# Three transformer blocks on one core: residual held token-major, with norm roots as columns per token block

## What is computed

```python
# block 1: modulated pre norm (scale and shift from c), gated post norm
h = rms_norm(x, g_pre) * (1 + scale) + shift
h = (silu(h @ w_gate) * (h @ w_up)) @ w_down            # or a mixer
x = x + 0.5 * (1 + gate) * rms_norm(h, g_post)          # factor 1 for the mixer
# block 2: plain pre norm, post norm
x = x + 0.5 * rmsnorm(swiglu_2(rmsnorm(x, pre), w_gu, w_down), post)
# block 3, twice: pre norm only
x = x + hybrid(rms_norm_3(x, g_mix)) @ w_out
x = x + (silu(h2 @ w_gate) * (h2 @ w_up)) @ w_down      # h2 = rms_norm_3(x, g_ffn)
return rms_norm_3(x, g_final)
```

## Time and profile before

| | us |
|---|---|
| median of 3 runs | 3627.2 (3626.7 to 3627.62) |
| span of the profiled execution | 3626.8 |
| PE busy | 3478.4 (96%) |
| DVE busy | 1965.9 (54%) |
| ACT busy | 1124.9 (31%) |
| POOL busy | 153.6 (4%) |

### The profile page before, as it was taken

One profiled execution on the slowest core, in us unless ns is written; L12 is line 12 of the kernel. 1 busy time (PEld: TensorE's weight loads), 2 busy tenths in 40 slices (PEclk: granted clock), 3 DMA queues, 4 the chain that ended last, 5 costly groups with the idle time before them and its releaser, 6 DMA issues. The chain is left out here.

```text
span 3626.8 us, 45721 instructions
## 1 busy us (share of the span) xinstructions
PE 3478.4 (96%) x18518; PEld 2717.8 (75%) x18518; DVE 1965.9 (54%) x2658; ACT 1124.9 (31%) x1482; POOL 153.6 (4%) x127
## 2 busy tenths in 40 slices
PE   9999999999999999998799999999999999999998
PEld 7887776688878887677578886666788866568886
DVE  6667545622344333988553435795534358953334
ACT  2222334422232223342332223335322233542222
POOL 0000000000000000000000000330000022200000
PEclk7999999999999999999899999999999999999999
DMA  6554231122222222210022222210222221112221
GB/s 244 185 183 172 81 108 40 55 104 93 93 81 94 103 93 102 75 65 4 13 82 93 99 98 78 74 70 24 89 96 93 98 88 70 47 47 93 99 98 70
DMA packets 47231, 325.75 MB, mean 90 GB/s; under 512 B 5232, under 2 KB 5488, under 8 KB 8688
## 3 DMA queue, kind: packets, MB, share of 16 engines
q1 hardware_dynamic: 41792, 290.10, 22.4%
q0 software_dynamic: 5296, 33.61, 2.6%
HBM read 321.59 MB, written 2.10 MB: 89 GB/s over the span
## 5 line engine op out<-in xcount | busy, mean ns | idle before, releaser
L2107 PE MATMUL PS<-HH,WH 128*128 128x512 f32 x2264 | 895.5, 396 | 21.5 <-DVE HL L2531 15.9
L2108 PE MATMUL PS<-HL,WH 128*128 128x512 f32 x2264 | 884.1, 391 | 0.0
L2109 PE MATMUL PS<-HH,WL 128*128 128x512 f32 x2264 | 884.1, 391 | 0.0
L2513 DVE TENSOR_TENSOR WL<-RAW,WH 128x2048 fp32r<-128x2048 f32 x264 | 613.6, 2324 | 497.8 <-ACT WH L2366 497.5
L2366 ACT ACTIVATE WH<-RAW 128x2048 fp32r<-128x2048 f32 x264 | 503.0, 1905 | 297.4 <-PE PS L2109 289.5
L2107 PEld LDWEIGHTS PS<-HH,WH 128*128 128x128 f32 x2264 | 426.6, 188 | 140.3 <-issue 33.7
L2109 PEld LDWEIGHTS PS<-HH,WL 128*128 128x128 f32 x2264 | 426.6, 188 | 90.2
L2108 PEld LDWEIGHTS PS<-HL,WH 128*128 128x128 f32 x2264 | 427.0, 189 | 87.6 <-issue 1.4
L2107 PE MATMUL PS<-AH,WH 128*128 128x512 f32 x1056 | 412.5, 391 | 3.3 <-DVE A L2579 3.0
L2108 PE MATMUL PS<-AL,WH 128*128 128x512 f32 x1056 | 411.7, 390 | 0.0
L2109 PE MATMUL PS<-AH,WL 128*128 128x512 f32 x1056 | 411.5, 390 | 0.0
(11 more groups left out here) (412 smaller groups left out, 3596.7 us busy)
## 6 DMA issues: line engine op xcount, KB each, us to landing
RAW<-in_w SPq DMA_DIRECT2D x264, 1024.0 KB, 4.8
E<-in_ada POOLq DMA_DIRECT2D x28, 1024.0 KB, 5.1
E<-in_ada SPq DMA_DIRECT2D x4, 1024.0 KB, 12.0
G<-in_ada SPq DMA_DIRECT2D x4, 1024.0 KB, 20.3
X<-in_x SPq DMA_DIRECT2D x1, 2048.0 KB, 14.1
out_x<-A SPq DMA_DIRECT2D x8, 256.0 KB, 2.1
G<-in_cos POOLq DMA_DIRECT2D x4, 256.0 KB, 3.4
G<-in_sin POOLq DMA_DIRECT2D x4, 256.0 KB, 3.6
```

The costliest lines, as they stand in the source:

```text
L2107: nc.tensor.matmul(out, wh, xh, start=start, stop=False)
L2108: nc.tensor.matmul(out, wh, xl, start=False, stop=False)
L2109: return nc.tensor.matmul(out, wl, xh, start=False, stop=stop)
L2513: nc.vector.tensor_tensor(WL[:, w % 2, :], RAW[:, w % 2, :], WH[:, w % 2, :].bitcast(F32), ALU.subtract).then_inc(w_lo, 1)
```

## The change

The residual is held token-major: XT, the same memory as X, is four blocks of 128 tokens by 1024 channels, and HG is the same for Y. Down and out units have 128 tokens of the activations as the stationary operand and 512 channels of the weights moving (part()), so that token block i collects in banks 2i and 2i + 1. The last two units (leave()) end block by block. Each block's norm root is one column ST: ACT squares with an accumulator, takes Ln and Exp of a column, DVE corrects the column. gained() multiplies the banks by the post gain as a row, add_out() adds to the residual, normed() scales by the pre root into HG; PE turns this back to channel-major by fp32 transposes (turn_tokens(), eight a block), and hi and lo of 256 tokens by 128 channels are made from the banks. enter() starts units 0 and 1 of every next sub-layer behind the turning of all four blocks. Gone are norm_added, keep_clock, entry, the deferred form and its scaling. Post gains now stand as rows along the free axis: POOL loads those that are inputs, and for f10, m1, f11, where the gate makes them, gain_rows() makes them from columns on PE and ACT copies them (gains()), for m1 and f11 behind units 0 and 1. POOL loads a second, token-major copy of the input x (2 MB) in f10. The gate and up banks are PS[4] to PS[7]. The order of the lows in m2's out units changes, and the output is stored token-major in four DMAs of 512 KB.

```diff
+OUT_ORDER = {"mix1": [2, 3, 0, 1, 4, 5, 6, 7], "mix2": [4, 5, 6, 7, 0, 1, 2, 3], "mix3": [2, 4, 0, 1, 5, 6, 7, 3]}
...
-            def keep_clock(n):
-                for _ in range(n):
-                    nc.tensor.matmul(PS[4 + (t("norms") + 1) % 2][:], ONES[:], CN[:, 0:S], start=True, stop=True)
...
-            def entry(w, s):
...
-                pe.wait_ge(x_done, KD * (s - 1) + (2 if post else 6))
-                for n, k in enumerate(entry_order(s)):
-                    pe.wait_ge(hl_done, t("hl") - KD + n + 1)
-                    for c in range(2):
-                        last = mm3(PS[c][:], wh[:, KD * c + k, :], wl[:, KD * c + k, :], xh[:, k, :], xl[:, k, :],
-                                   n == 0, n == KD - 1)
-                    if n == KD - 1:
-                        last.then_inc(w_used, 1)
-                    if post and n == 3:
...
+            def gain_rows(s, banks):
+                at = CV_POST[s]
+                for k in range(KD):
+                    last = nc.tensor.matmul(banks[k // 4][:, k % 4 * P:k % 4 * P + P], CV[:, at + k:at + k + 1].to_broadcast([P, P]),
+                                            IDENT, start=True, stop=True)
+                    if k % 4 == 3:
+                        last.then_inc(gains_made, 1)
+            def turn_tokens(i):
+                pe.wait_ge(xs_done, t("xs") + i + 1)
+                for k in range(KD):
+                    last = nc.tensor.transpose(turned_block(k, i % 2 * P, P), HG[:, i, k * P:(k + 1) * P], IDENT)
+                last.then_inc(turned, 1)
...
+            def part(src, w, i, tokens, begins, ends):
+                wh, wl = (x[:, w % 2, :].rearrange("p (k c) -> p k c", k=2) for x in (WH, WL))
+                for c in range(2):
+                    for n, (xh, xl) in enumerate(src):
+                        last = mm3(PS[2 * i + c][:], xh[:, tokens], xl[:, tokens], wh[:, n, c * S:(c + 1) * S],
+                                   wl[:, n, c * S:(c + 1) * S], begins and n == 0, ends and n == 1)
...
+            def leave(s, w, first, second, second_arrives):
+                post, onward = plan["subs"][s]["post"], s + 1 < len(plan["subs"])
+                def one(u, i):
+                    return part((first, second)[u], w + u, i, slice(i * P, (i + 1) * P), False, u == 1)
+                one(0, 3)
+                one(0, 0)
+                second_arrives()
+                one(1, 0)
+                one(0, 1)
+                one(1, 1)
+                one(0, 2).then_inc(w_used, 1)
+                one(1, 2)
+                if onward:
+                    block_used(1, post)
+                    turn_tokens(0)
+                one(1, 3).then_inc(w_used, 1)
+                if onward:
+                    turn_tokens(1)
+            def enter(s):
+                w, (xh, xl), post = t("w"), halves(s), plan["subs"][s - 1]["post"]
+                units = [[(0, PS[4])], [(0, PS[5]), (1, PS[6])]] if plan["subs"][s]["kind"] == "mix1" else \
+                    [[(0, PS[4]), (1, PS[5])], [(0, PS[6]), (1, PS[7])]]
+                block_used(2, post)
+                block_used(3, post)
+                pe.wait_ge(hl_done, t("hl") + KD)
+                turn_tokens(2)
+                turn_tokens(3)
+                if s == 1:
+                    for a in range(ADA - ADA_SLOTS, ADA):
+                        ada(a, bank=TAIL_BANK, base=2 * (ADA - ADA_SLOTS))
+                for n, banks in enumerate(units):
+                    unit_arrives(w + n)
+                    wh, wl = blocks(w + n)
+                    for k in range(KD):
+                        if n == 0:
+                            pe.wait_ge(hl_done, t("hl") + KD + k + 1)
+                        for c, bank in banks:
+                            last = mm3(bank[:], wh[:, KD * c + k, :], wl[:, KD * c + k, :], xh[:, k, :], xl[:, k, :],
...
+                if s in MADE:
+                    gain_rows(s, (PS[1], PS[2]) if plan["subs"][s]["kind"] == "mix1" else (PS[0], PS[1]))
...
-            def out_projection(order):
+            def out_projection(s, order, tokens, freed):
...
+                for u in range(2):
+                    arrives(u)
+                    for i in tokens if u == 0 else range(NT):
+                        if u == 0:
+                            freed(i)
+                        last = part(acts(u), w + u, i, slice(i * P, (i + 1) * P), u == 0, False)
+                    last.then_inc(w_used, 1)
+                arrives(2)
+                leave(s, w + 2, acts(2), acts(3), lambda: arrives(3))
...
-                    norm_added()
-                    keep_clock(8 if deferred(s + 1) else 6)
...
+            def gains(s):
+                for c, to in enumerate(GAINS[s]):
+                    act.wait_ge(gains_made, 2 * MADE.index(s) + c + 1)
...
+                def square_out(i):
+                    for c in range(2):
+                        out_wait(act, t, 2 * i + c)
+                        nc.scalar.activation(JUNK[0][:, c * S:(c + 1) * S], PS[2 * i + c][:], ACT.Square,
+                                             accum_out=stat(i, c)).then_inc(sqh_done, 1)
+                def root_out(i):
+                    act.wait_ge(sqh_done, t("sqh") + 2 * i + 2)
+                    chain(nc.scalar.activation(stat(i, 2), stat(i, 1), ACT.Identity, bias=EPS_COL, scale=1.0 / D))
+                    chain(nc.scalar.activation(stat(i, 3), stat(i, 0), ACT.Ln, bias=stat(i, 2), scale=1.0 / D))
+                    nc.scalar.activation(stat(i, 3), stat(i, 3), ACT.Exp, scale=-0.5).then_inc(root_begun, 1)
+                def square_in(i):
+                    act.wait_ge(x_done, t("x") + i + 1)
+                    nc.scalar.activation(JUNK[1], XT[:, i, :], ACT.Square, accum_out=stat(i, 8)).then_inc(sqx_done, 1)
...
+                def hi(n):
+                    half, k = n // KD, n % KD
+                    if k == 0:
+                        act.wait_ge(turned, t("turned") + 2 * half + 2)
+                    if k >= 4:
+                        act.wait_ge(hl_done, t("hl") + n - 3)
+                    to = halves(s + 1)[0][:, k, 256 * half:256 * half + 256]
...
+                        ins = nc.scalar.activation(to, turned_block(k, 0, 256), ACT.Copy, scale=col(nxt["pre"], k))
+                    ins.then_inc(hh_done, 1)
...
+                square_in(0)
+                if post:
+                    square_out(1)
+                    root_out(1)
+                square_in(1)
+                if onward:
+                    split(last_w)
+                if post:
+                    square_out(2)
+                    root_out(2)
...
+                    if not post:
+                        square_in(2)
+                    hi(0)
+                    hi(1)
+                    if post:
+                        square_out(3)
+                        root_out(3)
+                    for n in range(2, 6):
+                        hi(n)
+                    split(last_w + 1)
+                    hi(6)
...
-                def scale(u, i=0):
-                    dve.wait_ge(w_used, w + u + 1 + i)
-                    nc.vector.tensor_tensor(V[:], PS[2 * (u % 2)][:], R[:], ALU.mult).then_inc(gate_scaled, 1)
-                    if u:
-                        dve.wait_ge(act_ready, base + u + i)
-                    nc.vector.tensor_tensor(R0[:], PS[2 * (u % 2) + 1][:], R[:], ALU.mult).then_inc(up_scaled, 1)
...
+                def gained(i):
+                    if i == 0:
+                        gains_arrive(dve, s)
+                    for c in range(2):
+                        dve.wait_ge(sqh_done, t("sqh") + 2 * i + c + 1)
+                        nc.vector.scalar_tensor_tensor(HG[:, i, c * S:(c + 1) * S], PS[2 * i + c][:], factor, GAINS[s][c],
+                                                       ALU.mult, ALU.mult).then_inc(hg_done, 1)
...
+                def add_out(i):
+                    if not post:
+                        for c in range(2):
+                            out_wait(dve, t, 2 * i + c)
+                            to = XT[:, i, c * S:(c + 1) * S]
+                            ins = nc.vector.tensor_tensor(to, to, PS[2 * i + c][:], ALU.add).then_inc(hg_done, 1)
+                        dve.wait_ge(hg_done, t("hg") + 2 * i + 2)
+                        nc.vector.memset(stat(i, 14), 0.0).then_inc(x_done, 1)
+                        return
...
+                    chain(nc.vector.scalar_tensor_tensor(stat(i, 4), stat(i, 0), 1.0 / D, stat(i, 2), ALU.mult, ALU.add))
...
+                    root = newton(stat(i, 4), stat(i, 3))
...
+                    nc.vector.scalar_tensor_tensor(XT[:, i, :], HG[:, i, :], root, XT[:, i, :], ALU.mult, ALU.add).then_inc(x_done, 1)
+                def normed(i):
+                    dve.wait_ge(sqx_done, t("sqx") + i + 1)
...
+                    i_[0] = i
+                    root = newton(stat(i, 10), stat(i, 9))
...
```

(90 more changed lines are left out.)

672 lines of the change are left out of this document (320 added, 352 removed).

## The result

The changed kernel takes 3733.2 us (median of 4 runs, 3732.0 to 3737.3) against 3627.0 (4 runs): 1.0298 times as long, 95% interval 1.0283 to 1.0312. The forecast was slower, 3678 in a range of 3642 to 3716. The direction was right; the time is 55 over the point and 17 beyond the range.

A forecast was written before the change was run, and what follows sets the result against it. The prediction took the matmul engine (PE), busy 96% of the span, and the stretches where it stands as the bound. 3627 + 68.7 for the boundaries - 17.6 for the other parts gave 3678 us, range 3642 to 3716.

The forecast's parts named there:

- The doubt that the last paragraph kept: Forecast is wrong if out parts of 12 matmuls, activations held and weights moving, don't start 0.2273 us apart.
- The boundaries: Nine sub-layer boundaries: losses sum to 237.9 us after the change against 169.2 before, +68.7.
- The gain rows: In f11 and m1, unit 2 waits for its WL behind ACT's gain copies: 8.9 and 8.2 us.
- (a): Kernel end: 8.6 us behind the last matmul instead of 15.4, -6.8, bounds -4 and -8.
- (b): m2's out units: new order has the first low ready before the wait, -4.9; 0 if the wait moves.
- (c): f10's tail: 36 matmuls instead of 12 ahead of the ada-sum wait, clock not lost, -3.3, bounds 0 and -6.
- (d): Down 0's wait for the last activation in the four FFNs losing R scaling: -3.0, 0 if the split ends it.
- (e): Order of parts: m1's out -0.6, the two of mix3 +1.0, each within 1 either way.
- rival 2: Boundaries: transposes break the stretch so the clock doesn't fall, 24 us less, 3654; chance 0.09.
- rival 1: Boundaries: transposes don't bring the clock back, first unit begins cold, +24 us in nine boundaries, 3702; chance 0.20.
- Rival 4: m1 and f11: gain rows don't hold up unit 2, 17.1 and 4.4 of clock less, 3656; chance 0.06.
- Rival 3: Boundaries: chain behind T much shorter than DVE's order, no restart, 103 us less, 3575, faster than before; chance 0.05.

The follow-up runs named there:

- the old addresses: Changed kernel with 32 unused columns (128 bytes) behind PV, so CN, E and G lie where they lay in the kernel before; 3667.5 us, 1.0114 of before.
- The late rows: Changed kernel with the addresses of before (3667), gain rows of f11 made in its unit 19, not behind units 0 and 1; 3659.1 us.
- the run with the clock kept: Changed kernel with the addresses of before (3667), plus 20, 14 or 8 unread fp32 matmuls while PE waits for blocks 2 and 3; 3655.9 us.
- the last experiment: Changed kernel, addresses of before: WL splits behind block 3's scale, f11 gain rows late, 17, 12 or 8 dummy matmuls, m1 gain copies later on ACT; 3602.6 us, 0.993 of before.

## Why the forecast missed

**The step that failed** is in its first paragraph: a unit is 48 matmuls "that start 0.2273 us apart [...] before and after the change". It was read from one program and carried over to the other; in the changed kernel it is 0.2324 to 0.2332. The doubt that the last paragraph kept, on the parts with the weights moving, named a sign that did come true (0.2332), but these parts aren't the reason: the gate and up units are as slow, and with the old addresses the parts run at 0.2270. The removal of four vectors from the parameter table was part of the change, costed at nothing because no instruction hangs on it, and it cost 66 us.

Without that, with the addresses kept, the change costs 3667.5 - 3626.2 = 41 us where 51 was forecast. By its terms, read from that run (T to third unit: 51.72, 57.96, 42.70, 44.24, 42.77, 45.12, 38.57, 37.25, 38.68; its span is 3665.8, 39.0 over before):

- The boundaries, forecast +68.7. The nine windows sum to 399.0, 38.9 over before. Block 0's transposes ahead of T add 1.03 each, 9.3, and for m1 and f11 the restart behind the third unit's late start adds 2.8 and 2.7: +53.6. The shape was right: f20, m2, f21 and m30 lose 21.9, 23.5, 22.0 and 24.4 where 24.5 was said, f30, m31 and f31 17.8, 16.5 and 17.9 where 20.2 was said. Sizes were off. Eight transposes at full clock take 1.03, not 1.9. The prediction took two records for one transpose, but the 288 transposes of L2215 are 288 records, and the kernel before already had eight in 1.09 us (timeline of PE of before):

```profile
598.80 1.09 PE L369 MATMUL PS<-CN,G 128*128 128x128 f32 x8 [0.43 <-DVE G L485]
```

  The other size is the clock. Where it stayed low into the first unit it costs more than the 2.2: 1.6 in the turnings (3.65 in place of 2.1) and 1.6 to 2.1 in the first 24 matmuls. That 24.5 comes near in the boundaries that paid both (m30 24.4, m2 23.5) is in part luck: the four sets of transposes were taken 2.7 too long, the clock 1.2 too short, and the turning began 0.7 later than said. And the restart of the first unit came in six boundaries of nine only. Behind the block 3 entries DVE also has a wait of 2.0 us for ACT that the sum doesn't have, and reaches its scales at T + 10.0 where 11.0 was said.
- The gain rows, 8.9 and 8.2: from the end of unit 1 to the start of unit 2 they are 8.7 and 8.1. With the terms around them, into f11 39.9 for 39.3 and into m1 39.1 for 40.0. Right. The late rows gave 8.4 back where that experiment expected 7: the silu and the splits of unit 2, thought to remain, no longer keep PE waiting.
- (a) The end, forecast -6.8: in the changed kernel 3730.3 - 3721.9 = 8.4 remain, where 15.4 were. -7.0. Right.
- (b) m2's out units, forecast -4.9. The wait that it rested on is as it was, 5.4 us ahead of the first out matmul, so this step failed; timelines of PE of before (first row) and of after:

```profile
1777.66 2.07 PE L1583 MATMUL PS<-E,A 128*128 128x512 f32 x2 [12.90 <-DVE A L1925]
...
1834.13 2.08 PE L1598 MATMUL PS<-E,A 128*128 128x512 f32 x2 [8.31 <-DVE A L1940]
1841.63 0.77 PE L2136 MATMUL PS<-WH,HH 128*128 128x512 f32 x1 [5.42 <-DVE HL L2656]
```

  The rest of m2 from its third unit is 3.4 shorter all the same, without the transposes, because another wait shrank: the one for DVE in m2's own work, 12.9 before and 8.3 after (8.3 with the old addresses too). That the number comes near -4.9 is luck. What shortened this wait wasn't tested.
- (c) f10's tail, forecast -3.3: T comes 0.4 earlier with 1.0 of transposes in it, so -1.5. The wait of 6.2 for the ada sums is 0.3 in the changed kernel and 0.7 with the old addresses. The clock stayed up in the changed kernel, which was 0.50 before, but not with the old addresses, where it was 0.50 for 3.4 us right behind that place. Windows of all engines (PE, PEld, DVE, ACT, POOL busy, PEclk) of after and of the run with the old addresses:

```profile
314.70:318.70 4.00, 4.00 (x20) 3.25 (x18) 3.93 (x4) 0.00 (x0) 0.00 (x0) 1.00 0.81 287
...
320.50:323.50 3.00, 3.00 (x8) 2.32 (x8) 0.00 (x0) 0.00 (x0) 0.51 (x1) 0.50 0.91 371
```

- (d) the four FFNs without R scaling: 1.0 each in three and 0.9 in f31, for 0.74: right. (e) for the two of mix3 +1.2 for +1.0, for m1 -0.2 for -0.6.

The bounds of (a) to (e) add up to 17 up and 7 down as they are given, and not to the 11 and 8 that the range uses; with 17 the range would end at some 3722, and would still have missed.

**The rivals.** The clock fell (against rival 2) in every boundary: the 16 turnings take some 3.65 us behind the idle time, and 8 of them 1.03 at full clock. For rival 1, that transposes don't bring it back, speak six boundaries of nine in the run with the old addresses. There the granted clock was below 1.00 in the first unit, and the first 24 matmuls took 1.6 to 2.1 us more than their share (into m1 that figure also holds a wait for the lows: in the run with the clock kept, 1.7 remain there at 1.00). In three (into f20, f21 and m31) they took 0.1 more. Windows of all engines of that run: the idle time, the turnings and the start of the first unit into f20, and the same two stretches of work into f30:

```profile
1098.82:1108.82 10.00, 0.00 (x0) 0.00 (x0) 9.70 (x22) 6.58 (x13) 1.07 (x2) 0.50 0.50 159
1108.89:1112.19 3.30, 3.30 (x16) 3.10 (x16) 1.29 (x4) 0.00 (x0) 0.00 (x0) 0.50 0.56 238
1113.64:1118.64 5.00, 5.00 (x22) 4.14 (x23) 2.59 (x7) 3.17 (x7) 0.00 (x0) 1.00 0.02 3
...
2584.88:2588.18 3.30, 3.30 (x16) 3.25 (x16) 1.29 (x4) 0.00 (x0) 0.00 (x0) 0.50 0.55 233
2589.70:2593.50 3.80, 3.80 (x9) 3.03 (x10) 2.60 (x7) 3.17 (x7) 0.00 (x0) 0.50 0.02 4
```

Into f20 the clock came back with nothing but sixteen transposes behind 15 us of idle time. Which boundaries these are changes from run to run: in the changed kernel it is two, into f21 and f31. The rule of the Trainium skill ("TensorE: Matmul & The Clock Gate", Part 4: PE-mode transpose), that full clock doesn't engage for transpose-mode work, agrees with the six; it doesn't with the three. Rival 4 would have been true of another order on ACT, as the last experiment shows. Rival 3, the short chain, was what the kernel could have had: with the splits out of the way, the clock kept, the gains late and the old addresses it came out 0.7% faster than before.

## What to carry to other kernels

When a diff changes the size of any buffer, compare the start-to-start time of the main matmul in the two traces before anything else, and compare how its two operands lie to each other in the two layouts; test it by padding. Behind the last matmul of a stage, write down the vector engine's own order up to the operation that the matmul engine waits for, and move out of it everything that could run under the next transposes. Work that waits for a later product (the gain copies) mustn't stand ahead of a weight split on an in-order engine.

## What was not expected of the hardware

Two buffers that feed the matmul engine have a distance that matters. With E at 0 or 248 modulo 256 from WH the 128x512 fp32 matmul starts every 0.2267 us, with 120 or 184 every 0.2321 to 0.2334, at a granted clock of 1.00 in both cases. That is 2.5 to 2.9% of the spacing, and 1.7 to 2.1% of the kernel's time. With 120 it acts alike when E holds the moving operand (gate and up units) and when it holds the stationary one (the down units of the changed kernel). With 184 the matmuls of the kernel before that have E as the stationary operand lose less, at means of 0.2285 to 0.2303. Moving both by 128 bytes costs nothing, and the loss is there when no other engine and no DMA is at work.

A gap of 2.1 to 2.2 us in PE's work led to a fall of the clock five times and twice not. Sixteen transposes behind idle time were enough for full clock in three boundaries of nine.
